# Building a gate matrix in steps of 12 tokens on three engines instead of 16 tokens on two

## The reference

```python
def one(xb):                                  # per block of 128 tokens
    q = (xb @ wq).reshape(128, 8, 2, 128)     # 8 heads, two half keys
    s = einsum('thcd,hcnd->thcn', q, sub_keys)
    top_s, top_i = lax.top_k(s, 16)
    cand_s = top_s[:, :, 0, :, None] + top_s[:, :, 1, None, :]
    cand_i = top_i[:, :, 0, :, None] * 128 + top_i[:, :, 1, None, :]
    fs, fi = lax.top_k(cand_s, 16)            # 16 experts of 16384, per head
    g = softmax(fs)
    a = gelu(einsum('td,thkd->thk', xb, u[idx]))
    return einsum('thk,thkd->td', g * a, v[idx])
```

## Time and profile before

| what | value |
|---|---|
| median of 3 runs | 4336.51 us (4335.9 to 4338.79) |
| profiled execution, its own time | 4336.22 us |
| its span in the profile | 4334.4 us |
| PE busy | 3931.9 us (91%) |
| VectorE (DVE) busy | 3315.0 us (76%) |
| ScalarE (ACT) busy | 1683.0 us (39%) |
| GpSimd (POOL) busy | 783.7 us (18%), all but 0.4 us of it in issuing DMAs |

### The profile page before, as it was taken

One profiled execution on the slowest core, in us unless ns is written; L12 is line 12 of the kernel. 1 busy time (PEld: TensorE's weight loads), 2 busy tenths in 40 slices (PEclk: granted clock), 3 DMA queues, 4 the chain that ended last, 5 costly groups with the idle time before them and its releaser, 6 DMA issues. The chain is left out here.

```text
span 4334.4 us, 55420 instructions
## 1 busy us (share of the span) xinstructions
PE 3931.9 (91%) x20813; PEld 3285.9 (76%) x20813; DVE 3315.0 (76%) x6704; ACT 1683.0 (39%) x2864; POOL 783.7 (18%) x532
## 2 busy tenths in 40 slices
PE   6999998997799999999978898986369999999998
PEld 5554648997799999999943656586268999999997
DVE  2564815889799999999922434259979999999998
ACT  1113601119444444444423444221384444444443
POOL 0000000000233333333300000000003333333331
PEclk8999988969999999999989898998699999999999
DMA  4420013226999999999821010110179999999996
GB/s 175 155 88 29 1 59 112 79 98 195 380 414 414 401 406 407 404 402 406 361 112 41 1 39 1 59 54 1 58 228 421 415 411 400 407 406 405 402 406 280
DMA packets 234651, 1032.92 MB, mean 238 GB/s; under 512 B 15920, under 2 KB 117232, under 8 KB 126320
## 3 DMA queue, kind: packets, MB, share of 16 engines
q0 software_dynamic: 76032, 553.68, 31.7%
q1 hardware_dynamic: 158352, 475.70, 28.1%
HBM read 969.92 MB, written 59.39 MB: 237 GB/s over the span
## 5 line engine op out<-in xcount | busy, mean ns | idle before, releaser
L1324 POOL DMA_INDIRECT xT<-in_uv,rows x172 | 257.0, 1494 | 2359.4 <-POOLq L970 1916.0
L1324 POOL DMA_INDIRECT gbuf<-in_uv,rows x340 | 517.8, 1523 | 878.3 <-DVE hT L1491 808.5
L1491 DVE SCALAR_TENSOR_TENSOR hT<-gbuf,act,hT 128x1024 f32<-128x1024 f32 x336 | 416.8, 1282 | 6.0
L1476 DVE SCALAR_TENSOR_TENSOR gbuf<-gbuf,ht 128x1024 f32<-128x1024 f32 x340 | 401.9, 1218 | 6.2 <-DMA gbuf<-in_uv,rows 6.2
L100 PE MATMUL ps<-hT,ring 128*128 128x512 f32 (+1 forms) x624 | 325.1, 603 | 47.6 <-DMA ring<-in_wts 32.1
L1338 PE MATMUL ps<-h0h,U0h 128*128 128x384 f32 x1024 | 345.0, 337 | 10.6 <-DVE U0l L1450 10.6
L1338 PE MATMUL ps<-h1h,U1h 128*128 128x384 f32 x1024 | 345.0, 337 | 10.2 <-DVE U1l L1450 10.2
L1338 PE MATMUL ps<-h1h,U1l 128*128 128x384 f32 x1024 | 344.9, 337 | 0.0
L1338 PE MATMUL ps<-h0h,U0l 128*128 128x384 f32 x1024 | 344.7, 337 | 0.0
L1338 PE MATMUL ps<-h1l,U1h 128*128 128x384 f32 x1024 | 344.5, 336 | 0.0
L1338 PE MATMUL ps<-h0l,U0h 128*128 128x384 f32 x1024 | 344.3, 336 | 0.0
(11 more groups left out here) (339 smaller groups left out, 8974.3 us busy)
## 6 DMA issues: line engine op xcount, KB each, us to landing
ring<-in_u SPq DMA_DIRECT2D x128, 1024.0 KB, 12.6
ring<-in_v SPq DMA_DIRECT2D x128, 1024.0 KB, 9.3
ring<-in_wts SPq DMA_DIRECT2D x26, 2048.0 KB, 8.3
gates<-ring SPq DMA_DIRECT2D x24, 2048.0 KB, 7.6
ring<-gates SPq DMA_DIRECT2D x64, 768.0 KB, 16.1
xT<-in_ada_late SPq DMA_DIRECT2D x24, 1024.0 KB, 4.8
abuf<-in_ada_mid POOLq DMA_DIRECT2D x16, 1024.0 KB, 5.2
gbuf<-in_uv,rows POOLq DMA_INDIRECT x340, 10.1
```

Source lines behind the costliest of these rows:

```text
L1324: pool.indirect_dma_start(out=slots[m % GSLOTS], out_offset=None, in_=inp[f"uv{l}"], in_offset=bass.IndirectOffsetOnAxis(ap=rows[:, c:c + ...
L1476: v.scalar_tensor_tensor(u, u, 1.0, ht[:, m // P, :], ALU.mult, ALU.mult, accum_out=act4[:, n % 2, m % 2:m % 2 + 1]).then_inc(sem(n_ + "do ...
L1491: v.scalar_tensor_tensor(y, x, w, y, ALU.mult, ALU.add).then_inc(sem(n_ + "acc"), 1)
```

## The change

A step has 12 tokens instead of 16, so 32 steps per layer, and a store covers 24 tokens instead of 32. Of the 12 weighted one-hots, VectorE makes 2 directly, ScalarE scales 6, and GpSimd makes the last 4 with one tensor_scalar each, reading `iota` in SBUF. VectorE's comparisons and its 2 tensor_scalars read the ramp from a copy in PSUM bank 7, which ScalarE makes once per layer. PE's steps use banks 0 to 2 and 3 to 5 and wait for GpSimd too.

```diff
-BT = 32
+BT = 24
...
+        iota_ps = ps[:, 7, 0:P]
...
-        stage = ring[:, 0:2, :].rearrange("p b (g t k) -> p b g t k", g=GROUPS, t=BT)
-        SUB, DIRECT = 16, 6
+        stage = ring[:, 0:2, 0:GROUPS * BT * NG].rearrange("p b (g t k) -> p b g t k", g=GROUPS, t=BT)
+        SUB, DIRECT, SCALED = 12, 2, 6
...
                 def gate_step(r):
-                    b = 4 * (r % 2)
+                    b = 3 * (r % 2)
                     pe.wait_ge(sem("gm_one"), r + 1)
+                    pe.wait_ge(sem("gm_pool"), r + 1)
                     pe.wait_ge(sem("gm_scaled"), r + 1)
...
-                    for t in range(DIRECT, SUB):
+                    for t in range(DIRECT, DIRECT + SCALED):
...
-                    b, q = 4 * (r % 2), (r // 2) % 2
+                    b, q = 3 * (r % 2), (r // 2) % 2
...
-                    src = ps[:, b:b + 4, :].rearrange("p b (t n) -> p (b t) n", t=4)\
+                    src = ps[:, b:b + 3, :].rearrange("p b (t n) -> p (b t) n", t=4)\
...
+                act.copy(iota_ps, iota[:]).then_inc(sem("gm_iota"), 1)
                 evict_sel(0)
...
+            @block.gpsimd
+            def _(pool):
+                for r in range(STEPS):
+                    t0 = r * SUB
+                    pool.wait_ge(sem(n_ + "selT"), (t0 + SUB - 1) // P + 1)
+                    if r >= 2:
+                        pool.wait_ge(sem("gm_mm"), r - 1)
+                    for t in range(DIRECT + SCALED, SUB):
+                        last = pool.tensor_scalar(one2[:, r % 2, t, :], iota[:], selT[:, 1, t0 + t:t0 + t + 1],
+                                                  selT[:, 2, t0 + t:t0 + t + 1], ALU.is_equal, ALU.mult)
+                    last.then_inc(sem("gm_pool"), 1)
...
-                    v.wait_ge(sem(n_ + "selT"), r // 8 + 1)
+                    v.wait_ge(sem("gm_iota"), 1)
+                    v.wait_ge(sem(n_ + "selT"), (t0 + SUB - 1) // P + 1)
...
-                    n = SUB - DIRECT
-                    v.tensor_tensor(one2[:, r % 2, DIRECT:], selT[:, 1, t0 + DIRECT:t0 + SUB].unsqueeze(2).to_broadcast([P, n, P]),
-                                    iota[:].unsqueeze(1).to_broadcast([P, n, P]), ALU.is_equal).then_inc(sem("gm_eq"), 1)
+                    n = SCALED
+                    v.tensor_tensor(one2[:, r % 2, DIRECT:DIRECT + n],
+                                    selT[:, 1, t0 + DIRECT:t0 + DIRECT + n].unsqueeze(2).to_broadcast([P, n, P]),
+                                    iota_ps.unsqueeze(1).to_broadcast([P, n, P]), ALU.is_equal).then_inc(sem("gm_eq"), 1)
                     for t in range(DIRECT):
-                        v.tensor_scalar(one2[:, r % 2, t, :], iota[:], selT[:, 1, t0 + t:t0 + t + 1],
+                        v.tensor_scalar(one2[:, r % 2, t, :], iota_ps, selT[:, 1, t0 + t:t0 + t + 1],
                                         selT[:, 2, t0 + t:t0 + t + 1], ALU.is_equal, ALU.mult)
-                    v.tensor_tensor(one1[:, r % 2], selT[:, 0, t0:t0 + SUB].unsqueeze(2).to_broadcast([P, SUB, P]),
-                                    iota[:].unsqueeze(1).to_broadcast([P, SUB, P]), ALU.is_equal)\
+                    v.tensor_tensor(one1[:, r % 2, 0:SUB], selT[:, 0, t0:t0 + SUB].unsqueeze(2).to_broadcast([P, SUB, P]),
+                                    iota_ps.unsqueeze(1).to_broadcast([P, SUB, P]), ALU.is_equal)\
                      .then_inc(sem("gm_one"), 1)
```

## The result

The changed kernel takes 4294.59 us in the median of 4 runs (4292.35 to 4298.69), the kernel before 4337.65 us (4 runs). The ratio is 0.9903, 95% interval 0.9887 to 0.9918: 1.0% faster. The profiled execution took 4292.35 us, its span is 4290.5 us. The kernel before had 4334.4, so 43.9 us went.

What follows compares the result with a forecast made beforehand. VectorE was taken to bound the gate stage. Per layer, 123.4 us becomes 101.8 (−21.6), + 1.05 start-up, − 2.5 at the end: −23.1; twice −46, so 4336.2 − 46.2 = 4290 us, range 4280 to 4297.

Steps and rivals of the forecast that it cites:

- 0.867, 0.65 and 1.667: VectorE's us per gate step: comparison of 6 scaled tokens, two tensor_scalars, 12-token comparison; together 3.18 us.
- the upper bound of 0.324 us: VectorE's tensor_scalar reading the ramp from PSUM: taken at 0.324 us each, against a lower bound of 0.257.
- rival three: Gate step: four PSUM reads 0.065 us dearer, or ScalarE losing time at hand-offs; 3.44 us a step, 4307; chance 0.10.
- Just hidden: Loop of VectorE and PE through the two-deep buffers: 6.34 us per two steps, under 2 × 3.18.
- The estimate of 0.5 us an instruction: GpSimd's one-hots in the gate step: 0.5 us each, four a step, hidden, worth 0 in the sum.
- the bound that the prediction gave for being hidden: GpSimd's four one-hots a gate step stay hidden up to 0.79 us each.
- The chances: GpSimd as the gate stage's bound: chance 0.05 for 0.80 to 0.94 us an instruction, 0.09 above 0.98.
- 1.5 and 2.0: Start of the gate stage: VectorE's wait in us for PE at low clock, layers 0 and 1; 1.05 us more.
- my 19.2: Gate stores: ns per 384 B piece, making 4.9 us a store, hidden behind the steps.
- rival two: 384 B gate stores bound the stage: if pieces cost twice, 12 us a store, 67 us more a layer, 4470; chance 0.08.
- One of its signs: Gate stores as bound would show in ScalarE's copy waiting for a store and a tail over 8 us.
- 1.2 off: End of the gate stage: the last store takes 1.2 us less a layer.

Runs made afterwards that it cites:

- run 5: Against the kernel before: steps of 12, no GpSimd, VectorE makes 4 directly, ScalarE scales 8, ramp in PSUM; 4347.7 us, ratio 1.0029.
- run 4: Against the kernel before: steps of 12, no GpSimd, VectorE makes 4 directly, ScalarE scales 8, ramp in SBUF; 4333.1 us, ratio 0.9992.
- run 3: Changed kernel, but VectorE's two tensor_scalars read the ramp from SBUF, its tensor_tensors still from PSUM; 4294.9 us.
- run 6: Changed kernel, but three tokens for GpSimd and three direct ones for VectorE; 4313.1 us, ratio 0.9944.
- run 7: Changed kernel, but five tokens for GpSimd and one direct one for VectorE; 4330.1 us.
- run 8: Changed kernel with useless extra matmuls ahead of PE's first gate step, 2 in layer 0 and 5 in layer 1; 4292.6 us, ratio 0.9903.
- run 10: Changed kernel with run 9's moved store wait, and GpSimd's expert row gathers held until the first U has landed; 4295.8 us, ratio 0.9908.
- run 11: The changed kernel itself measured again, nothing altered; 4294.9 us, ratio 0.9901.
- run 1: Changed kernel, but all of VectorE's comparisons and its two tensor_scalars read the ramp from SBUF; 4496.1 us, ratio to before 1.038.
- run 2: Changed kernel, but VectorE's two tensor_tensors read the ramp from SBUF, its tensor_scalars still from PSUM; 4499.1 us.
- run 9: Changed kernel, but the wait for the last gate store moved from the choice block to before the expert block's first gate load; 4293.6 us, ratio 0.9901.

## Why the prediction was right, and where its terms were off

Forecast 4290, measured 4294.6; the sum was −46.2 us, the spans differ by −43.9. The cause was as stated: the step of the gate stage, 5.14 us for 16 tokens before and 3.20 for 12 now, where the forecast had 3.18. What sets those 3.20 us is not what the prediction named.

- **VectorE per step.** The forecast's 0.867, 0.65 and 1.667 are 0.87, 0.64 and 1.66 in the rows. The value taken for a tensor_scalar from PSUM, the upper bound of 0.324 us, is what run 5 shows (0.32). The tensor_tensors cost nothing more from PSUM, by L384 and L385 in the prediction and by runs 4 and 5 (1.75 and 1.76 us for 1536 elements). The fixed 65 ns more from PSUM that the Trainium skill's table (VectorE: DVE Perf Modes, the section on the TRN2 errata) gives did not appear. Of rival three, the half on dearer PSUM reads is out.
- **The hand-off.** "Just hidden" was wrong by a little: two steps take 6.40 us where VectorE's work alone is 6.34. And the loop that has no slack is not VectorE's, which the prediction closed, but ScalarE's, which it did not. In the rows of the middle step PE ends at 1018.36 (1015.44 + 2.92), ScalarE's copy starts 0.03 later, the scaling 1.34 after the copy, the last scaling ends 1.86 later at 1021.59, PE starts 0.25 after it and runs 2.92: 6.40. The 0.25 to 0.26 from ScalarE's end to PE's start are the shortest in any run here, and run 3 shows them with nothing else near. VectorE's loop has room: PE starts 0.06 after the end of VectorE's last comparison in the kernel before and in runs 4, 5 and 6, but 0.09 here, and with 0.06 that loop is 6.37. The profile puts PE's wait down to VectorE, whose comparison ends last (1020.01 + 1.75 = 1021.76), but ScalarE's hand-off takes longer. So the other half of rival three, ScalarE with 0.07 us of room losing time at each hand-off, came true for 0.02 us a step, 0.6 us a layer. Run 3 fits: VectorE got faster and the step stayed. A run that changes ScalarE's share alone was not made.
- **GpSimd.** The estimate of 0.5 us an instruction was wrong: it is 0.79 long and 0.77 start to start, and the bound that the prediction gave for being hidden was 0.79. It is still worth 0 in the sum, but its own loop (0.18 from PE's end, 3.11 for four, 0.10 to PE as in run 7, 2.92) is 6.31 of the 6.40, a cover of 0.05 us a step, and in a few steps PE does wait for it (0.52 us at 1070.12). That it stayed hidden was luck: the prediction's bounds were 0.23 and 1.49, and it came out 0.02 under the edge. The chances should have been less one-sided; runs 6 and 7 show both slopes.
- **The start.** VectorE's third step waits 2.69 and 2.64 us where I had 1.5 and 2.0. I took the 3.0 and 3.9 us at the low clock from the trace of before; here they are 5.0 in layer 0 (from 971.41 to 976.4) and 5.7 in layer 1 (from 3080.29). 0.9 us a layer. Windows of the changed kernel, two of layer 0 and one of layer 1; the last number but two is the clock:

```profile
975.40:976.40 1.00, 1.00 (x6) 1.00 (x6) 0.00 (x0) 0.00 (x0) 0.00 (x0) 0.50 0.00 0
976.40:977.40 1.00, 1.00 (x11) 1.00 (x10) 0.50 (x1) 0.60 (x1) 0.45 (x1) 0.93 0.00 0
...
3085.00:3086.00 1.00, 1.00 (x7) 1.00 (x7) 0.12 (x1) 0.22 (x1) 0.07 (x1) 0.52 0.00 0
```

- **The stores.** 384-byte pieces stream at about 290 to 320 GB/s, about 5.2 us a store or 20 ns a piece, against my 19.2 and the 23.7 of a 512-byte piece. No short piece costs double, and rival two is out as a bound. One of its signs did show, small: in the profiles of runs 3, 8, 10 and 11 ScalarE's copy waits 0.4 to 1.0 us in all for a store. And the landing fell only from 7.6 to 7.1 us and the tail (last copy's end to the next block) from 8.0 to 7.4 us in layer 0 and to 7.9 in layer 1, where I took 1.2 off: 0.6 to 1.1 us a layer. Page of the changed kernel, then windows of it while a store runs:

```profile
gates<-ring SPq DMA_DIRECT2D x32, 1536.0 KB, 7.1
```
```profile
1022.00:1023.00 1.00, 1.00 (x10) 1.00 (x10) 1.00 (x3) 1.00 (x2) 1.00 (x2) 1.00 1.18 322
1023.00:1024.00 1.00, 1.00 (x11) 1.00 (x11) 1.00 (x3) 1.00 (x5) 1.00 (x2) 1.00 1.26 290
```

0.6 + 0.9 + 0.9 = 2.4 us a layer: 23.1 forecast, 20.7 measured. The rest of the difference, 2.6 us in the other direction, lies outside the stages, within the scatter there; that it fell towards the forecast is luck.

What the prediction did not weigh is what happens without the PSUM ramp. It read that edit as a cost only; runs 1 and 2 show that with this split it is the condition for the whole gain. For this forecast it made no difference, since the change had it.

## What to carry to other kernels

Where VectorE bounds a stage of small one-hots, GpSimd can take a share at 0.77 us for 128 x 128 f32, if no tensor_tensor of VectorE beside it has both inputs in SBUF: put the constant one in PSUM. Sum each engine's starts per step, and then close the loop through the double buffers once for every engine that PE waits for. Here VectorE, ScalarE and GpSimd have 3.17, 3.10 and 3.10 us of work a step, and the longest loop is ScalarE's, whose hand-off to PE takes 0.25 us where VectorE's takes 0.06. And before a wait at a block's end is moved, look at what the loads behind it would share the DMA engines with: here 7 us earlier brought nothing.

## What the runs showed that I had not expected

- The conflict is one-sided: with the ramp in SBUF VectorE's rows keep their length (0.96 and 1.75 us) and GpSimd's go from 0.79 to 1.37 us on average. Two steps go from 6.40 to 13.38 us in the rows shown. GpSimd's own loss is 4.5 us of that (10.76 against 6.3); 2.2 more are PE's (8.0 against 5.8), whose clock is at 0.50 (1.2 GHz) after each gap of 5.2 us and for the first 5 us of the next burst.
- VectorE's tensor_scalars from SBUF did not slow GpSimd at all (0.792 us against 0.791); VectorE was held, by some 0.08 us in the median instruction.
- A load issued behind a running store took 3.91 us to issue instead of 0.35, and ScalarE began on it 14.3 us after its issue instead of 4.8 (run 9, layer 0).
- ScalarE's last scaling reaches PE 0.25 us after its end, VectorE's comparison 0.06 and GpSimd's instruction 0.10: an engine with less work a step than another can still set the step.
